# Memory attention on high and low parts, and operand tiles at 64 modulo 128 bytes

## What is computed

```python
def memory_cross_attention(x, mem, norm_g, mem_g, wq, wk, wv, wo):
    h = rms_norm(x, norm_g)
    m = rms_norm(mem, mem_g)
    q = (h @ wq).reshape(B_, S, MEM_HEADS, MEM_HEAD_DIM)
    k = (m @ wk).reshape(B_, M, MEM_HEADS, MEM_HEAD_DIM)
    v = (m @ wv).reshape(B_, M, MEM_HEADS, MEM_HEAD_DIM)
    logits = jnp.einsum('bshd,bmhd->bhsm', q, k) * (MEM_HEAD_DIM ** -0.5)
    p = jax.nn.softmax(logits, axis=-1)
    o = jnp.einsum('bhsm,bmhd->bshd', p, v)
    return o.reshape(B_, S, MEM_HEADS * MEM_HEAD_DIM) @ wo
```

## Time and profile before

| | |
|---|---|
| median of three executions | 1057.9 us (1056.57 to 1059.49) |
| profiled execution | 1059.27 us |
| span of its trace | 1057.5 us |
| mean granted clock of TensorE | 0.998 |
| instructions in the trace | 18974 |

### The profile page before, as it was taken

One profiled execution on the slowest core, in us unless ns is written; L12 is line 12 of the kernel. 1 busy time (PEld: TensorE's weight loads), 2 busy tenths in 40 slices (PEclk: granted clock), 3 DMA queues, 4 the chain that ended last, 5 costly groups with the idle time before them and its releaser, 6 DMA issues.

```text
span 1057.5 us, 18974 instructions
## 1 busy us (share of the span) xinstructions
PE 1050.6 (99%) x7296; PEld 972.6 (92%) x7296; DVE 860.9 (81%) x1077; ACT 664.9 (63%) x940; POOL 2.7 (0%) x8
## 2 busy tenths in 40 slices
PE   9999999999999999999999999999999999999998
PEld 8888998888888999999899999999899889999998
DVE  6789986487778846898998778798998899878786
ACT  6566654366555447666787767675546688667673
POOL 0000000000000000000000000000000000000000
PEclk9999999999999999999999999999999999999999
DMA  9952463354555554534555555454333565555531
GB/s 347 228 195 81 159 236 123 120 187 169 181 190 198 196 207 154 190 125 155 206 192 199 203 177 185 163 209 168 122 123 117 174 225 192 185 194 193 198 125 75
DMA packets 30527, 186.88 MB, mean 177 GB/s; under 512 B 3735, under 2 KB 6520, under 8 KB 8840
## 3 DMA queue, kind: packets, MB, share of 16 engines
q1 hardware_dynamic: 29896, 185.05, 50.2%
q10 hardware_dynamic: 576, 1.05, 0.3%
HBM read 183.96 MB, written 1.34 MB: 175 GB/s over the span
## 4 chain that ended last, share of the span: by engine, by line
PE 97%; DVE 1%; DMA 1%; ACT 0%; SPq 0%; issue 0%; DVEq 0%
PE g L527 61%; PE d L527 36%; PE d L530 1%; DMA raw<-weights 1%; DVE w_lo L1497 0%; DVE scores L1501 0%; DVE row_max L1584 0%; PE g L530 0%; DVE b_both L1497 0%; SPq L453 0%; DVE hy_conv L1501 0%; ACT hy_probs_t L1037 0%; DVE hy_conv L1491 0%; DVE qkv L1491 0%; ACT w_hi L1037 0%
## 5 line engine op out<-in xcount | busy, mean ns | idle before, releaser
L1497 DVE TENSOR_TENSOR w_lo<-raw,w_hi 128x2048 fp32r<-128x2048 f32 (+1 forms) x175 | 389.5, 2227 | 64.8 <-ACT w_hi L1037 64.5
L527 PE MATMUL g<-a_both,w_hi 128*128 128x256 f32 (+1 forms) x1568 | 406.2, 335 | 1.1 <-DVE w_lo L1497 0.8
L1037 ACT ACTIVATE w_hi<-raw 128x2048 fp32r<-128x2048 f32 (+1 forms) x174 | 324.8, 1870 | 80.7 <-PE d L527 47.7
L527 PE MATMUL g<-a_both,w_lo 128*128 128x256 f32 x1136 | 320.4, 282 | 0.0
L527 PEld LDWEIGHTS g<-a_both,w_hi 128*128 128x128 f32 x1568 | 267.9, 191 | 33.2 <-DVE w_lo L1497 3.5
L527 PEld LDWEIGHTS g<-a_both,w_lo 128*128 128x128 f32 x1136 | 216.8, 191 | 0.1
L527 PE MATMUL g<-b_both,w_hi 128*128 128x256 f32 (+1 forms) x720 | 168.4, 311 | 0.4 <-DVE b_both L1497 0.4
L527 PE MATMUL d<-hid_hi,w_lo 128*128 (+1 forms) x528 | 148.7, 282 | 0.0
L527 PE MATMUL d<-hid_hi,w_hi 128*128 (+1 forms) x528 | 148.7, 282 | 0.0
L527 PE MATMUL d<-hid_lo,w_hi 128*128 (+1 forms) x528 | 148.7, 282 | 0.0
L527 PEld LDWEIGHTS g<-b_both,w_hi 128*128 128x128 f32 x720 | 118.2, 191 | 8.9 <-DVE b_both L1497 0.6
(11 more groups left out here) (318 smaller groups left out, 1409.8 us busy)
## 6 DMA issues: line engine op xcount, KB each, us to landing
raw<-weights SPq DMA_DIRECT2D x168, 1024.0 KB, 4.8
bias_tab<-bias_dram SPq DMA_DIRECT2D x8, 192.0 KB, 10.6
x<-x_t ACTq DMA_DIRECT2D x4, 256.0 KB, 5.3
raw<-weights SPq DMA_DIRECT2D x4, 256.0 KB, 6.3
raw<-weights SPq DMA_DIRECT2D x2, 512.0 KB, 7.4
mem_t<-mem_t SPq DMA_DIRECT2D x1, 1024.0 KB, 9.7
out<-x SPq DMA_DIRECT2D x3, 256.0 KB, 2.2
hy_swap<-hy_qk SPq DMA_DIRECT2D x4, 128.0 KB, 6.2
```

Source lines behind the costliest of these rows:

```text
L527: return pe.matmul(out, lhsT, rhs, start=start, stop=stop, skip_group_check=True)
L1037: return act.activation(out, in_, func, **kw)
L1497: return dve.tensor_tensor(out, a, b, ALU.subtract)
```

## The change

It makes keys, queries, values and probabilities of memory attention pairs of a high and a low part. ACT copies a bank to the high part (pair_hi, value_hi, counted by the new semaphore bank_hi), DVE subtracts for the low part (pair_lo, values_lo, probs_lo) and counts the bank as evicted. Each plain float32 product becomes three float32r matmuls. Keys and queries are left unscaled; rstd_mem is multiplied in where the scores are drained, the queries' rstd goes as a column (q_scale, turned by TensorE ahead of the last query chunk) into the exponential and, negated, into the maximum. The order of the weight splits around these steps moves with them. And x, a_both, b_both, the small tiles, H and TR move on by 64 bytes; inside these regions mem_k, mem_v and scores_mem move on by another 64, so that they are back at a multiple of 128, as the weights are. The core of the diff:

```diff
+        assert place["at"] % 128 == 0, place["at"]
+        place["at"] += 64
         x = sb("x", [KT, T])
         a_both = sb("a_both", [KT, 2, T], F32R)
...
+        q_scale = sb("q_scale", [TT])
+        q_negated = sb("q_negated", [TT])
...
-        H = place["at"]
+        H = (place["at"] + 63) // 128 * 128 + 64
...
-        mem_v = at("mem_v", H + 16 * KB, [TT, DM])
+        mem_v = (at("mem_v_hi", H + 16 * KB + 64, [TT, DM], F32R), at("mem_v_lo", H + 24 * KB + 64, [TT, DM], F32R))
+        probs_m = (at("probs_m_hi", H + 44 * KB, [4, 512], F32R), at("probs_m_lo", H + 8 * KB, [4, 512], F32R))
...
-        mem_k = at("mem_k", TR + 12 * KB, [KT, T])
+        mem_k = (at("mem_k_hi", TR + 12 * KB + 64, [KT, T], F32R), at("mem_k_lo", TR + 64, [KT, T], F32R))
...
-        q_mem = at("q_mem", H + 24 * KB, [KT, T])
+        q_mem = (at("q_mem_hi", H + 24 * KB, [KT, T], F32R), at("q_mem_lo", H, [KT, T], F32R))
...
-        scores_mem = at("scores_mem", H + 32 * KB, [8, T])
+        scores_mem = at("scores_mem", H + 32 * KB + 64, [8, T])
...
-            outputs("w_cq", C)
+            for j in range(COUNT["w_cq"]):
+                if j == COUNT["w_cq"] - 1:
+                    turn_scale(rstd, FIRST_OUT["w_cq"] + 1)
+                chunk("w_cq", j, j % U, C, fresh=j == 0)
+                if j == 1:
+                    norm_sum()
             for h in range(4):
                 pe.wait_ge(evicted, FIRST_OUT["w_cq"] + h + 1)
                 acquire(h)
                 for t in range(TT):
                     for d in range(2):
-                        last = mm(D[h][:, t * T:(t + 1) * T], q_mem[:, 2 * h + d, t * P:(t + 1) * P], mem_k[:, 2 * h + d, :],
-                                  d == 0, d == 1)
+                        q_hi, q_lo = (part[:, 2 * h + d, t * P:(t + 1) * P] for part in q_mem)
+                        k_hi, k_lo = (part[:, 2 * h + d, :] for part in mem_k)
+                        to = D[h][:, t * T:(t + 1) * T]
+                        mm(to, q_hi, k_hi, d == 0, False)
+                        mm(to, q_hi, k_lo, False, False)
+                        last = mm(to, q_lo, k_hi, False, d == 1)
                 fill(h, last, full_dve, drained_dve)
...
-                turned[h] = fill(h % 2, last, full_act, drained_act)
+                turned[h] = fill(h % 2, last, full_act, drained_dve)
...
-                    mm(to, mem_v[:, 0, v], probs_t[:, h, 0:T], True, False)
-                    last = mm(to, mem_v[:, 1, v], probs_t[:, h, T:2 * T], False, True)
+                    for t in range(TT):
+                        v_hi, v_lo = (part[:, t, v] for part in mem_v)
+                        p_hi_t, p_lo_t = (part[:, h, t * T:(t + 1) * T] for part in probs_m)
+                        mm(to, v_hi, p_hi_t, t == 0, False)
+                        mm(to, v_hi, p_lo_t, False, False)
+                        last = mm(to, v_lo, p_hi_t, False, t == 1)
...
+            def pair_hi(name, j, to):
+
+                act.wait_ge(chunk_done, FIRST[name] + j + 1)
+                fn(flat(to[:, 2 * j:2 * j + 2, :]), G[(FIRST_OUT[name] + j) % U][:]).then_inc(bank_hi, 1)
...
             act.wait_ge(mixed_ready, count.next(mixed_ready))
             hi_parts(A, 0, [att_a[:, f, :] for f in range(4)], [pcol("moba_out_g", f) for f in range(4)])
             ahead("w_ck", 1, 1)
+            pair_hi("w_ck", 0, mem_k[0])
+            pair_hi("w_ck", 1, mem_k[0])
             rough_rstd(2 * T)
...
             for b in range(2):
                 act.wait_ge(mixed_ready, count.next(mixed_ready))
                 hi_parts(A, 4 + 2 * b, [att_b[:, 2 * b + f, :] for f in range(2)], [subln_g[:, 0:1]] * 2)
+            pair_hi("w_ck", 2, mem_k[0])
             ahead("w_ck", 3, 0)
+            pair_hi("w_ck", 3, mem_k[0])
             residual("w_out", C, "cross_norm_g")
...
             opening("w_cq")
+            pair_hi("w_cq", 0, q_mem[0])
+            pair_hi("w_cq", 1, q_mem[0])
             for j in range(2, COUNT["w_cq"]):
                 ahead("w_cq", j, j % U)
+                pair_hi("w_cq", j, q_mem[0])
             ahead("w_cv", 0, 0)
-            exps(scores_mem, 0, 8, slice(0, T))
+            act.wait_ge(max_done, count.next(max_done))
+            for m in range(8):
+                last = fn(scores_mem[:, m, :], scores_mem[:, m, :], ACT.Exp, bias=neg_max[:, 0, m:m + 1],
...
+            def value_hi(j):
+
+                act.wait_ge(chunk_done, FIRST["w_cv"] + j + 1)
+                for t in range(TT):
+                    fn(mem_v[0][:, t, (j - 1) * 2 * P:(j + 1) * 2 * P], G[(j - 1 + t + FIRST_OUT["w_cv"]) % U][:],
+                       scale=rstd_mem_tok[:, t:t + 1]).then_inc(bank_hi, 1)
+
             for j in range(1, COUNT["w_cv"]):
                 ahead("w_cv", j, j % U)
+                if j == 1:
+                    value_hi(1)
             for step in range(5):
                 if step < 4:
-                    from_bank(probs_t[:, step, :], D[step % 2][:])
+                    act.wait_ge(full_act, count.next(full_act))
+                    fn(probs_m[0][:, step, :], D[step % 2][:]).then_inc(bank_hi, 1)
+                if step == 1:
+                    value_hi(3)
...
+            def pair_lo(name, j, parts):
+
+                dve.wait_ge(bank_hi, count.next(bank_hi))
+                hi, lo = (flat(part[:, 2 * j:2 * j + 2, :]) for part in parts)
+                sub(lo, G[(FIRST_OUT[name] + j) % U][:], hi.bitcast(F32)).then_inc(evicted, count.one(evicted))
+
             def mem_keys(j, split=True):
-                evict("w_ck", j, j % U, pair_at(mem_k, j), rstd_mem, split=split)
-
-            def mem_values(j):
-                ahead("w_cv", j, j % U)
-                if j % 2 == 1:
-                    evict_tokens("w_cv", j, mem_v[:, :, (j - 1) * 2 * P:(j + 1) * 2 * P], rstd_mem_tok)
+                if split:
+                    ahead("w_ck", j, j % U)
+                pair_lo("w_ck", j, mem_k)
+
+            def values_lo(j):
+
+                for t in range(TT):
+                    dve.wait_ge(bank_hi, count.next(bank_hi))
+                    hi, lo = (part[:, t, (j - 1) * 2 * P:(j + 1) * 2 * P] for part in mem_v)
+                    bank = G[(j - 1 + t + FIRST_OUT["w_cv"]) % U]
+                    fused(lo, bank[:], rstd_mem_tok[:, t:t + 1], hi.bitcast(F32), ALU.mult, ALU.subtract).then_inc(evicted, count.one(evicted))
+
+            def probs_lo(h):
+
+                dve.wait_ge(bank_hi, count.next(bank_hi))
+                sub(probs_m[1][:, h, :], D[h % 2][:], probs_m[0][:, h, :].bitcast(F32)).then_inc(drained_dve, count.one(drained_dve))
...
-            for j in range(COUNT["w_cq"]):
-                evict("w_cq", j, j % U, pair_at(q_mem, j), split=j > 1)
+            pair_lo("w_cq", 0, q_mem)
+            pair_lo("w_cq", 1, q_mem)
+            pair_lo("w_cq", 2, q_mem)
+            ahead("w_cq", 2, 2)
+            dve.wait_ge(full_dve, count.next(full_dve))
+            dve.tensor_scalar(q_negated[:], D[STAT][:, 0:T:P], -0.0625, None, ALU.mult).then_inc(dve_own, count.one(dve_own))
+            dve.tensor_scalar(q_scale[:], D[STAT][:, 0:T:P], 0.0625, None, ALU.mult).then_inc(drained_dve, count.one(drained_dve))
+            pair_lo("w_cq", 3, q_mem)
+            ahead("w_cq", 3, 0)
             for b in range(4):
                 dve.wait_ge(full_dve, count.next(full_dve))
-                dve.tensor_scalar(scores_mem[:, b:8:4, :], as_tiles(D[b][:]), 0.0625, None, ALU.mult).then_inc(drained_dve, count.one(drained_dve))
+                mul(scores_mem[:, b:8:4, :], as_tiles(D[b][:]), over(rstd_mem[:], 2)).then_inc(drained_dve, count.one(drained_dve))
             dve.wait_ge(drained_dve, count.sent[drained_dve])
-            negate_max(scores_mem, 0, slice(0, T))
-            mem_values(0)
+            dve.tensor_reduce(row_max[:, 0, 0:8], scores_mem[:], AX_X, ALU.max).then_inc(dve_own, count.one(dve_own))
+            dve.wait_ge(dve_own, count.sent[dve_own])
+            mul(as_tiles(neg_max[:, 0, :], 4), as_tiles(row_max[:, 0, :], 4), along(q_negated[:], 4)).then_inc(max_done, 1)
+            ahead("w_cv", 0, 0)
...
-            for j in (1, 2, 3):
-                mem_values(j)
+            ahead("w_cv", 1, 1)
+            values_lo(1)
+            for j in (2, 3):
+                ahead("w_cv", j, j % U)
+            for h in range(2):
+                probs_lo(h)
+            values_lo(3)
             for h in range(4):
+                if h >= 1 and h < 3:
+                    probs_lo(h + 1)
```

More of the change, by code:

```diff
@@ L207, in program @@
         inv_freq = const[:, C_FREQ:C_FREQ + 1]
-        H = place["at"]
+        H = (place["at"] + 63) // 128 * 128 + 64
         H_SIZE = 52 * 1024
         TR = H + H_SIZE
-        assert TR + 20 * 1024 <= nc.sbuf_usable_end, (TR + 20 * 1024, nc.sbuf_usable_end)
+        assert TR + 20 * 1024 + 64 <= nc.sbuf_usable_end, (TR + 20 * 1024, nc.sbuf_usable_end)
         KB = 1024
@@ L332, in program @@
         mixed_ready = sem("mixed_ready")
```

(23 more changed lines are left out.)

## The result

| | before | after |
|---|---|---|
| median of 20 executions each | 1057.75 us (1056.57 to 1059.97) | 1063.15 us (1058.85 to 1065.87) |
| ratio | | 1.0047, 95% interval 1.0040 to 1.0055 |
| profiled execution, span | 1059.3, 1057.5 | 1065.2, 1063.3 |
| mean granted clock | 0.998 | 0.997 |

The account below looks back on a forecast made before the run. The prediction took TensorE's matmul spacing to bound the kernel. From the median 1057.9 us it added +1.3 for memory attention and -23 for the new addresses, giving 1036 us, with a range from 1004 to 1064.

Parts of the forecast that it names:

- what bounds the kernel: Whole kernel: TensorE, busy 1050.6 of 1057.5 us and 97% of the chain, so spacing of matmuls sets the time.
- memory attention on TensorE: Memory attention: float32r matmuls save 1.2 us on scores and 1.2 on values, q_scale's transposes add 0.2; together -2.2 us.
- memory attention's order: Key copies on ACT ahead of DVE's low parts: means of att_b late, TensorE waits in w_out; +3.1 us, from 0 to +5.
- The probabilities' wait: Memory attention: turned probabilities go ACT, DVE, TensorE, only the last head's low part late; +0.4 us, between 0 and 1.5.
- the +1.3 of the sum: Memory attention as a whole: -2.2 + 3.1 + 0.4 = +1.3 us, between -2 and +5.
- the new addresses, -23: Nearly all float32r matmuls: one side of each product moved on by 64 bytes quickens the pace, -23 us.
- I take half of the 46: Address term: the 64-byte shift undoes half of the possible 46 us of slower pace, giving -23 us.
- the sums of 46 and 54 us: Whole possible address relief: 5184 matmuls of 256 columns at 5.5 or 7 ns, 1488 of 512 at 12 ns.
- The tests that I named for it: Address term: forecast wrong if pace moves in one family only, or if the 512 columns keep their 228 ns.
- rival 2: All 6672 float32r matmuls: reading 64 bytes off costs 1.4 ns each, 9 us, so 1068 us; chance 0.18.
- Rival 1: Whole kernel: addresses change nothing, only the memory part counts; 1059 us, or 1056 to 1063; chance 0.27.
- Rival 3: Whole kernel: relief is whole and another engine takes over; 1005 to 1013 us, rather 1015; chance 0.15.

Follow-up runs that it names:

- e3: e2 with ACT's copies of key banks and DVE's low parts moved forward; 1063.15 us, ratio 1.0041 to the kernel before.
- e5: e3 with q_scale and q_negated behind TR and no pad, so H and TR lie at the bytes of before; 1057.08 us, ratio 0.9990.
- e1: Kernel before with the new addresses alone, memory attention left plain float32; 1060.49 us, ratio 1.0017.
- e10: Kernel before with a_both moved by 128 bytes, b_both by 640, H by 896, all multiples of 128; 1063.11 us beside 1060.12 of before.
- e9: Kernel before with weights (raw, w_hi, w_lo) moved by 64 bytes and all activations by 128; 1057.24 us beside 1060.12 of before.
- e11: e5 with weights at 64 modulo 128, a_both and b_both at 96, H at the bytes of e9; 1051.73 us, ratio 0.9929.
- e8: The changed kernel run again, unchanged, for a second trace; 1065.23 us beside 1058.45 of before.
- e4: Kernel before with a_both, H and TR 32 bytes past a multiple of 128 and b_both 96 past; 1059.48 us beside 1058.87 of before.
- e2: The changed kernel with x, a_both, b_both, H and TR back at multiples of 128 bytes; 1066.05 us, ratio 1.0071 to before.
- e7: Kernel before with raw, w_hi, w_lo, a_both, b_both, H and TR all 64 past a multiple of 128; 1062.1 us beside 1058.45.
- e6: Changed kernel in e3's order, a_both and b_both 32 bytes past a multiple of 128, H and TR 64 past; 1052.01 us, ratio 0.9952.

## Why the prediction was wrong, point by point

**Right: what bounds the kernel**, and that it is as long as its matmuls are apart. What the addresses did was decided by 1 to 5 ns in a spacing of 120.

**Right: memory attention on TensorE.** Forecast -1.2 for the scores: 6.91 to 5.65. Values: the two heads that stand whole on the chain take 1.37 and 1.42 us for 12 matmuls where the earlier trace rows had 1.73, for four heads -1.3. The two transposes for q_scale: 0.22, as forecast.

**Right: memory attention's order.** mean_sq at 114.42 (forecast 114.5), the first low part at 126.13 (126.35), the wait 2.1 (2.0). From the first matmul of w_out to the first of w_cq the second trace of after has 25.96 us, before 22.80: +3.2 where the sum had +3.1; taking the order away in e3 gave 3 us back. ACT's copy took 0.48 on the chain, not 0.6. The probabilities' wait was 0.2, not 0.4. The part as a whole: e5 gives -1.1 to -1.4 with the order mended, so some +2 with it, and after against e1 gives +3.2, beside the +1.3 of the sum. The DVE step behind ACT's copy came late by what stood ahead of that copy (mean_sq at 114.42 for 112.08); that was to be read from the earlier trace rows, and it was.

**Wrong: the new addresses, -23.** The step that failed is "I take half of the 46". Of the 6 ns that 119.8 stands above the 113.8 of the earlier trace rows, the 64 bytes undid 2 in chunks of three matmuls (119.8 to 117.5, 6.5 us with hid), which is near the kind of relief I took; hid alone gave only 0.8 (118.6 to 117.8). But I carried it over to the pairs and to chunk_tokens, where the same 64 bytes cost: 348.0 to 353.3 and 228 to 233.3, 7.8 us. The earlier trace rows had shown the forms apart, 119.9 with one and 346.9 with the other, and nothing in my argument gave a sign for the forms with 512 columns. No run shows the 12 ns at 512 columns and the 7 at 256 that the sums of 46 and 54 us take. What the runs showed in their place: 512 columns with weights moving at 227.8 to 233.3 ns, the pairs at 346.7 to 353.3, chunks of three at 114.9 to 120.0. That a shift undoes half of the 46 was my estimate. The bounds of that term should have reached as far above nothing as below it in each form by itself. The tests that I named for it, a pace that moves "in one family only (a_both but not hid)" and 512 columns that "keep their 228", left out what came: a_both and hid both fell, and the 512 columns of chunk_tokens rose from 228 to 233.

Deeper lies a premise that I didn't state: that a family has a pace, which the remainder modulo 128 decides. The earlier trace rows held a sign against it, 119.9 ns from a_both and 118.5 from hid with both at a multiple of 128, and I used it only as the price of rival 2. e10 changes no remainder and loses 3.0 us; e3 and e5 differ in 128 bytes of H and in 5.4 us; e9 and e11 run down0 at 113.9 and 118.2 from the same bytes; e8 runs one chunk of an unchanged program at 113.3 and 117.9. What can be said: where weights and activations lie 64 apart, chunks of three stand at 117.3 to 117.8 (or 113 to 115, when it so happens), pairs at 349 to 353; 32 apart, 117 to 118 and 347 (hid up to 119.5); 96 apart (e4 alone), 118.3 and 353; equal, 118.6 to 120, and 348 to 352. Inside a band e8 and the turns of e9 suggest that the start of the stream has a part; no run was made to tell, and I can't say by what rule. Nor does any run show what in the hardware sets the pace. The 5.5 ns at 256 columns were the distance to the earlier trace rows, the row with weight loads of 16 columns, and e9's down0 runs at 113.9 ns with loads of 128: the size of the load alone doesn't make that distance.

The traces answer one more rival, that the other engines' work at the moved bytes slows TensorE. In before the distance between matmuls from hid is 118.6 ns while DVE is busy throughout and 118.8 while it stands idle; in e2 both are 119.9. With DMAs in flight or none it is 118.7 and 118.5, and 120.0 and 119.9. The step from before to e2 is there in either case.

**The rivals.** Rival 1 (nothing, 1059) holds for the plain float32 products that stood for it: the sums of squares take 1.73 us for 8 with the ones 64 bytes off (before) and at the same remainder as the squares (e1), and keys against queries, at equal remainders each time, 6.91 for 32 in before, e1, e4, e7, e9 and e10. For the float32r products it doesn't: with e3's list of instructions, placement alone made 1051.7 to 1063.2 us (e3, e5, e6, e11), and e5 against e3 shows 5.4 us for 128 bytes of H and what lies with it. Rival 2 (dearer, 1068) had the right sign; its price, 1.4 ns on all matmuls, was the spread between a_both's and hid's chunks of three, and both of these fell; only the pairs and chunk_tokens rose, and the mean spacing by 1.3 us / 6672 = 0.2 ns. Rival 3 didn't come.

**Not in the forecast at all: the clock.** One more stretch at a granted clock of 0.50, 1.7 us, in both profiled executions of after and, by their mean clocks, in at most half of its 20. In the first trace of after it begins 1.5 us after TensorE's wait of 2.1 us near 124; in the second that wait is followed by none, and the stretch near 440 that before has too is there. In before that one begins at 440.2; from 437.2 to 439.8 TensorE ran products of 2 and 8 moving columns. The stretch near 739 begins some 2.5 us after a wait of 0.2 us for gla_lr in both traces, and e9 has one near 732, without such a wait, but none near 440. The traces of e5 and e6 have none, those of the other kernels one. Two traces don't show that the change brings it, and no run here was made to tell.

**Open.** What decides between 113, 118 and 120 ns at equal addresses, and why a pair of 512 and 256 columns answers to a shift with the other sign than three of 256. For the difference between e1 (1.0017, with a pace of -0.9 in its one trace) and what its pace alone would give, some 2.5 us, I have no row either; its executions ran from 1058.3 to 1063.2.

## What to carry to other kernels

Where TensorE is never starved, an edit that adds a small tile moves every operand behind it, and that alone was worth 5.4 us in 1058 here: put new tiles at the end, keep the others at their bytes, and only then read what the edit itself does (e3 against e5). Try placements by measuring the whole kernel, form by form, rather than by reasoning from one form to another: e6 and e11 came out of paces that had been seen, and even so one family in e11 ran otherwise. And where an eviction is split between ACT and DVE, count what stands ahead of it in ACT's list: moving the copies forward was worth 3 us.

## What the runs showed of the hardware that I had not expected

- The spacing of float32r matmuls of 256 columns with 128-column weights often takes one of a few values, near 113.5, 118 and 120 ns, and holds it for whole chunks: in e9 all of down0 runs at 113.9, and the pieces of ffn1 alternate between 5.45 and 5.65 us (113.5 and 117.7 ns); in e2 hid stands at 119.9. hid's 118.6 in before is no such value but the mean of single distances between 114 and 122. The means of the pairs are 347 to 353.
- A pace can differ between two executions of one program (113.3 and 117.9 ns in the last chunk of hy_out), while the sums over the kernel agree to 0.2 us.
- A move of a region by 128 bytes changed the pace of products that read another region: the pairs from a_both run at 352.3 ns in e3 and 348.0 in e5, with a_both and the weights at the same bytes.
